# Paged softmax attention in a one-core decoder layer: values multiplied under each key block's own maximum, block weights applied in the fold

## The reference

```
gate  = q . mean(k of a block of 256 keys)      # 4 past blocks = 2 pages each
sel   = top_3(gate)  plus the query's own token
s     = q . k * 64**-0.5, masked to sel
p     = softmax(s over all chosen keys)
o     = sum(p * v)
```

## Time and profile before

| | us |
|---|---|
| median of 3 runs | 596.98 |
| lowest, highest | 594.94, 605.13 |
| the profiled execution | 596.88 |
| its span, first to last instruction | 594.9 |
| mean granted clock of PE | 0.947 of full |
| PE, DVE, ACT, POOL busy | 534.4, 350.0, 163.5, 56.6 |

### The profile page before, as it was taken

One profiled execution on the slowest core, in us unless ns is written; L12 is line 12 of the kernel. 1 busy time (PEld: TensorE's weight loads), 2 busy tenths in 40 slices (PEclk: granted clock), 3 DMA queues, 4 the chain that ended last, 5 costly groups with the idle time before them and its releaser, 6 DMA issues.

```text
span 594.9 us, 10233 instructions
## 1 busy us (share of the span) xinstructions
PE 534.4 (90%) x3943; PEld 450.2 (76%) x3943; DVE 350.0 (59%) x548; ACT 163.5 (27%) x230; POOL 56.6 (10%) x126
## 2 busy tenths in 40 slices
PE   7879997997998888988789689987999999999997
PEld 5557775675688766865564059887999999999996
DVE  4540269478798787955734537465665566455441
ACT  4101010811132122211000224364343443424420
POOL 6800010000104800000101000000000000000000
PEclk8979897997699999999969899998999999999999
DMA  9996356476049467643739998595465655645201
GB/s 294 332 302 207 108 189 218 123 204 221 19 150 324 144 221 245 217 132 119 244 111 376 384 352 268 173 298 163 148 209 162 195 169 168 195 144 193 73 19 37
DMA packets 98998, 116.79 MB, mean 196 GB/s; under 512 B 6317, under 2 KB 81278, under 8 KB 98934
## 3 DMA queue, kind: packets, MB, share of 16 engines
q1 hardware_dynamic: 93218, 104.42, 54.8%
q10 hardware_dynamic: 3908, 7.42, 3.5%
q0 software_dynamic: 1824, 4.30, 2.6%
HBM read 113.30 MB, written 2.99 MB: 195 GB/s over the span
## 4 chain that ended last, share of the span: by engine, by line
PE 64%; DVE 21%; DMA 7%; ACT 3%; issue 3%; ACTq 1%; SPq 0%; DVEq 0%
PE bank L336 61%; DVE prod L916 5%; DVE s_all L1019 5%; DVE mats L916 3%; DMA ring<-in_ada_w_dram 2%; DMA ring<-in_w_out_dram 2%; DVE BTP L916 1%; DVE cv L1127 1%; DMA ring<-in_cache_v_dram 1%; DMA x_nat<-in_x_sample_dram 1%; PE bank L373 1%; PE bank L382 1%; ACT w_part L1692 1%; DMA qb<-q_rows_dram 1%; PE bank L517 1%
## 5 line engine op out<-in xcount | busy, mean ns | idle before, releaser
L336 PE MATMUL bank<-a_hi,w_part 128*128 128x264 f32 x832 | 153.5, 286 | 2.1 <-DVE a_lo L1464 2.1
L916 DVE TENSOR_TENSOR w_part<-ring,w_part 128x2048 fp32r<-128x2048 f32 (+1 forms) x38 | 84.9, 2236 | 89.2 <-ACT w_part L1692 89.2
L336 PEld LDWEIGHTS bank<-a_hi,w_part 128*128 128x128 f32 x832 | 129.8, 189 | 2.6 <-issue 2.6
L336 PE MATMUL bank<-a_lo,w_part 128*128 128x264 f32 x416 | 118.4, 285 | 0.0
L1692 ACT ACTIVATE w_part<-ring 128x2048 fp32r<-128x2048 f32 (+1 forms) x38 | 70.9, 1871 | 86.0 <-PE bank L336 75.0
L336 PE MATMUL bank<-hT,ring 128*128 128x264 f32 x352 | 85.7, 406 | 0.8 <-ACT proj L1555 0.8
L336 PEld LDWEIGHTS bank<-hT,ring 128*128 128x128 f32 x352 | 70.0, 201 | 14.9 <-issue 2.4
L336 PEld LDWEIGHTS bank<-a_lo,w_part 128*128 128x128 f32 x416 | 79.0, 190 | 0.1
L336 PE MATMUL bank<-hid_hi,w_part 128*128 128x264 f32 x352 | 64.9, 285 | 0.0
L336 PEld LDWEIGHTS bank<-ident 128*128 128x128 f32 x362 | 48.1, 212 | 10.4 <-issue 5.6
L336 PEld LDWEIGHTS bank<-hid_hi,w_part 128*128 128x128 f32 x352 | 54.5, 188 | 0.1
(11 more groups left out here) (326 smaller groups left out, 570.3 us busy)
## 6 DMA issues: line engine op xcount, KB each, us to landing
ring<-in_ada_w_dram SPq DMA_DIRECT2D x24, 1024.0 KB, 7.3
ring<-in_cache_k_dram SPq DMA_DIRECT2D x64, 256.0 KB, 3.6
ring<-in_w_in_dram SPq DMA_DIRECT2D x11, 1024.0 KB, 5.6
ring<-in_w_gate_dram SPq DMA_DIRECT2D x11, 1024.0 KB, 5.3
ring<-in_w_up_dram SPq DMA_DIRECT2D x11, 1024.0 KB, 5.3
ring<-in_cache_v_dram SPq DMA_DIRECT2D x40, 256.0 KB, 4.2
ring<-in_w_down_dram SPq DMA_DIRECT2D x8, 1024.0 KB, 5.1
ring<-in_cache_v_dram ACTq DMA_DIRECT2D x24, 256.0 KB, 5.2
```

What stands on the lines that cost most here:

```text
L336: return pe.matmul(out, lhsT, rhs, start=start, stop=stop, skip_group_check=True)
L916: return v.tensor_tensor(out, a, b_, op)
```

## The change

The queries are handled in two groups of four. For each group, as soon as its scores exist (`G0`, `G1`), PE transposes and sums them, and DVE makes the diagonal of maxima and the blocks' gates. `DMAX0`, `DMAX1`: every block's own maximum is subtracted from its scores, with no mask and no maximum over blocks, and ACT writes the exponentials straight into the strips (`p_own`), a query's 8 columns at a place of their own in the 32. So the values of four queries gather in one bank (`pv0`, `pv1`), block by block, since a half now holds each block's first or second page. The masks and folds of `V` are gone, ACT copies each of the two banks, and ACT issues no pages. The ranking of blocks (minimum of four gates in place of counts), the maximum over blocks, the denominators and one factor for each block, query and head follow in `DEN`. `WC` turns the factors into columns, and `FO` multiplies the gathered values by them in sixteen small products that write the transposed result. In `ORDER`, `A7` moves behind `UD`, `A8` ahead of `G1` and `OWN`, and `A9` behind `V1`.

```diff
+    GS = NS // 2
+    GW = GS * NPG * H
+    XW = NPG * 32 + H
...
-             "H0 QB6 K11 L4 M4 H1 A5 H2 L5 K12 M5 A6 QB7 H3 K13 H4 L6 K14 M6 POOL H5 UA A7 K15 H6 UB UC H7 UD A8 HE OWN "
-             "A9 DMAX DEXP V0 XA V1 XB V2 XC V3 XD V4 MX V5 V6 MW0 V7 VE MD MW1").split()
+             "H0 QB6 K11 L4 M4 H1 A5 H2 L5 K12 M5 A6 QB7 H3 K13 H4 L6 K14 M6 POOL H5 UA G0 K15 H6 DMAX0 UB UC H7 UD A7 HE "
+             "A8 G1 OWN V0 DMAX1 V1 A9 XA V2 XB V3 XC V4 XD DEN V5 MX WC V6 MW0 V7 FO MD MW1").split()
...
+            def group_sums(g):
+                if g:
+                    keep_awake(6, 8)
+                pe.wait_ge(sem("k_scored"), GS * (g + 1))
+                b = opened(f"gsT{g}", (3, 6)[g])
+                for n in range(2):
+                    o = g * GW + n * P
+                    pe.transpose(b[:, GW + n * P:GW + (n + 1) * P], s_all[:, o:o + P], ident[:, :])
+                closed(mm(b[:, 0:GW], ones[:, :], s_all[:, g * GW:(g + 1) * GW]), f"gsT{g}")
+
+            def spread_max(g):
+                if g:
+                    keep_awake(5, 2)
+                pe.wait_ge(sem("max_diag"), g + 1)
+                b = opened(f"pmax{g}", (3, 5)[g])
+                closed(mm(b[:, 0:GW], ones[:, :], w_a[:, g * GW:(g + 1) * GW]), f"pmax{g}")
 
             def page_values(q):
-                if q == 0:
-                    keep_awake(4, 9)
-                    pe.wait_ge(sem("p_ready"), 1)
-                b = opened(f"pv{q}", 4 + q % 2)
+                g, j = q // GS, q % GS
+                if j == 0:
+                    pe.wait_ge(sem("p_ready"), g + 1)
+                    opened(f"pv{g}", (7, 4)[g])
+                b = bank[(7, 4)[g]]
                 for hf in range(HALVES):
                     slot = arrived(pe, ("v", (q, hf))).rearrange("p (k n) -> p k n", k=PGI)
-                    for k in range(PGI):
-                        last = mm(b[32 * k:32 * k + 32, :], pP[:, q * NPG + hf * PGI + k, :], slot[:, k, :],
-                                  hf == 0, hf == HALVES - 1)
+                    for k in range(NB):
+                        last = mm(b[32 * k:32 * k + 32, :], pP[g][:, j * NPG + PPB * k + hf, :], slot[:, k, :],
+                                  j + hf == 0, j == GS - 1 and hf == HALVES - 1)
...
+            def turn_weights():
+                pe.wait_ge(sem("wgt"), 1)
+                b = opened("wcol", 5)
+                for g in range(2):
+                    last = mm(b[:, g:g + 1], w_a[:, g * P:(g + 1) * P], ident[:, 0:1])
+                closed(last, "wcol")
+
+            def fold():
+                keep_awake(6, 6)
+                pe.wait_ge(sem("selw"), 1)
+                pe.wait_ge(sem("pv_rows"), 2)
+                b = opened("y8", 6)
+                for g in range(2):
+                    for c in range(AC):
+                        for h2 in range(2):
+                            r = 64 * h2
+                            last = mm(b[r:r + 64, c * NS + g * GS:c * NS + (g + 1) * GS],
+                                      pv_out[g][:, c * P + r:c * P + r + 64], selw[:, g, 2 * c + h2, :])
+                closed(last, "y8")
...
+            def spread_max(g):
+                b = full(v, f"pmax{g}")
+                freed(v.tensor_reduce(of(top4, g), b[:, 0:GW].rearrange("p (n t h) -> p n h t", t=PPB, h=H), AX, ALU.max),
+                      f"pmax{g}")
+                v.wait_ge(bank_free[filled[f"pmax{g}"][0]], frees_at(f"pmax{g}"))
+                s = paged(s_all[:, g * GW:(g + 1) * GW])
+                inc(tt(s, s, bc(of(top4, g).unsqueeze(2), [P, GS * NB, PPB, H]), ALU.subtract), "shifted")
+
+            def block_weights(_):
+                wide = [P, NS, NB, H]
+                low, top = sm64[:, 0, :, :], sm64[:, 1, :, :]
+                own, own_e, den, own_w = (sm64[:, n, :, :] for n in range(2, 6))
+                v.wait_ge(bank_free[filled["gsT1"][0]], frees_at("gsT1"))
+                step(v.tensor_reduce(low, over_blocks(gate4[:, :, :, :]), AX, ALU.min))
+                step(tt(cnt4[:, :, :, :], gate4[:, :, :, :], bc(low.unsqueeze(2), wide), ALU.is_le))
+                step(tt(cnt4[:, :, :, :], cnt4[:, :, :, :], bc(bidx[:, :, :].unsqueeze(1), wide), ALU.mult))
+                step(v.tensor_reduce(low, over_blocks(cnt4[:, :, :, :]), AX, ALU.max))
+                step(tt(gate4[:, :, :, :], cnt4[:, :, :, :], bc(low.unsqueeze(2), wide), ALU.is_lt))
+                step(v.tensor_scalar(cnt4[:, :, :, :], gate4[:, :, :, :], FAR, -FAR, ALU.mult, ALU.add))
+                step(tt(cnt4[:, :, :, :], cnt4[:, :, :, :], top4[:, :, :, :], ALU.add))
+                step(v.tensor_reduce(low, over_blocks(cnt4[:, :, :, :]), AX, ALU.max))
+                step(tt(top, low, own, ALU.max))
+                tt(own_e, own, top, ALU.subtract)
+                step(tt(cnt4[:, :, :, :], top4[:, :, :, :], bc(top.unsqueeze(2), wide), ALU.subtract))
+                inc(v.tensor_scalar(cnt4[:, :, :, :], cnt4[:, :, :, :], 0.0, None, ALU.min), "w_shifted")
                 b = full(v, "den")
...
+                v.wait_ge(sem("w_exp"), 1)
+                step(tt(cnt4[:, :, :, :], cnt4[:, :, :, :], gate4[:, :, :, :], ALU.mult))
+                step(tt(sum4, sum4, cnt4[:, :, :, :], ALU.mult))
+                step(v.tensor_reduce(den, over_blocks(sum4), AX, ALU.add))
+                step(tt(den, den, own_e, ALU.add))
+                step(v.reciprocal(den, den))
+                tt(own_w, own_e, den, ALU.mult)
+                for g in range(2):
+                    q = slice(g * GS, (g + 1) * GS)
+                    last = tt(w_a[:, g * P:(g + 1) * P].rearrange("p (n j h) -> p j n h", n=NB, h=H), cnt4[:, q, :, :],
+                              bc(sm64[:, 4, q, :].unsqueeze(2), [P, GS, NB, H]), ALU.mult)
+                inc(last, "wgt")
...
+            def page_exps(g):
+                a.wait_ge(sem("shifted"), g + 1)
+                a.wait_ge(sem("p_zeroed"), g + 1)
+                s = s_all[:, g * GW:(g + 1) * GW].rearrange("p (j n h) -> p j n h", n=NPG, h=H)
+                inc(a.activation(p_own[g], s, ACT.Exp, scale=SCALE), "p_ready")
...
+            def pv_rows(q):
+                if q % GS == GS - 1:
+                    take(f"pv{q // GS}", pv_out[q // GS], P, AW, "pv_rows")
...
-                    load_pages(sp, it, range(PGI // 2 if kind == "v" and i[0] >= 2 else PGI))
+                    load_pages(sp, it, range(PGI))
```

More of the change, by code:

```diff
@@ L249, in load_pages @@
             kind, (q, hf) = item
-            first = q * NPG + hf * PGI
-            pages = [eng.value_load(table[0:1, first + k:first + k + 1], min_val=0, max_val=NPHYS - 1) for k in part]
+            index = [q * NPG + (PPB * k + hf if kind == "v" else hf * PGI + k) for k in part]
+            pages = [eng.value_load(table[0:1, n:n + 1], min_val=0, max_val=NPHYS - 1) for n in index]
             if item in before:
@@ L758, in page_values @@
+                    if j < GS - 1 or hf < HALVES - 1:
                         used_up(last, ("v", (q, hf)), "pe_read")
[L759 to L772, removed]
+                if j == GS - 1:
+                    closed(last, f"pv{g}")
+                    read_by(f"pv{g}", ("v", (q, HALVES - 1)))
@@ L1333, in own_scores @@
-                step(v.tensor_scalar(g4, c4, float(min(TOPK, NB + 1)), None, ALU.is_lt))
-                step(v.tensor_scalar(c4, g4, FAR, -FAR, ALU.mult, ALU.add))
-                b = full(v, "sT")
-                freed(v.tensor_reduce(tokmax[:, :], b[:, :].rearrange("p (n t) -> p n t", n=4), AX, ALU.max), "sT")
-                v.wait_ge(bank_free[4], frees_at("sT"))
-                v.wait_ge(sem("tails_out"), 64)
-                for n in range(4):
-                    last = v.tensor_scalar(w_a[:, n * P:(n + 1) * P], ident[:, :], tokmax[:, n:n + 1], None, ALU.mult)
@@ L1353, in denominators, with of, over_blocks, group_sums @@
-            def denominators(_):
-                v.wait_ge(sem("exp8"), 1)
-                inc(tt(paged(w_b), paged(w_b), bc(g4.unsqueeze(2), [P, NS * NB, PPB, H]), ALU.mult), "exps")
+                v.wait_ge(bank_free[filled["own"][0]], frees_at("own"))
+            def of(m, g):
+                return m[:, g * GS:(g + 1) * GS, :, :].rearrange("p q n h -> p (q n) h")
+            def over_blocks(m):
+                return m.rearrange("p q n h -> p q h n")
+            def group_sums(g):
+                if g == 0:
+                    v.wait_ge(sem("tails_out"), 64)
+                b = full(v, f"gsT{g}")
+                step(v.tensor_reduce(tokmax[:, 2 * g:2 * g + 2], b[:, GW:2 * GW].rearrange("p (n t) -> p n t", n=2), AX, ALU.max))
+                for n in range(2):
+                    o = g * GW + n * P
+                    last = v.tensor_scalar(w_a[:, o:o + P], ident[:, :], tokmax[:, 2 * g + n:2 * g + n + 1], None, ALU.mult)
+                inc(last, "max_diag")
+                freed(v.tensor_reduce(of(gate4, g), b[:, 0:GW].rearrange("p (n t h) -> p n h t", t=PPB, h=H), AX, ALU.add),
```

(16 more changed lines are left out.)

162 lines of the change are left out of this document (46 added, 116 removed).

## The result

| | before | after |
|---|---|---|
| median of 4 runs, us | 597.76 | 608.97 |
| lowest, highest | 594.94, 605.13 | 607.53, 614.03 |
| the profiled execution | 596.88 | 609.32 |
| its span | 594.9 | 607.6 |
| mean granted clock of PE | 0.947 | 0.917 |

The ratio is 1.0197, with a 95% interval of 1.0147 to 1.0246: 11.2 us slower, where 10.3 us faster was predicted. The range ended at 592.5. Whether the change is more than 2% slower, this interval leaves open.

What follows compares the result with a forecast made beforehand. The bound was taken as serial: softmax weights, then value pages at full DMA rate, then masks, folds and turn. Projection start moves from 356.07 to 345.8, 10.3 us earlier, so 596.88 becomes 586.6 us; range 580.5 to 592.5.

Steps and rivals of the forecast that it cites:

- Up to K15: Group 0's work placed behind UA: K15 starts at 263.4 in place of 265.07, 1.7 us earlier.
- V0 and A9: Values and turn before XA: V0 1.93 us, 0.6 added for the clock; XA starts at 302.5, 6.0 us earlier.
- XA to the mixer's sums: Delta mixer on PE with V2 to V4 between: sums done 15.5 us after XA starts, at 318.0.
- Roots and mixer: Behind the sums: table load hidden, roots end at 318.6, mixer ready at about 323.7, 11.2 us earlier.
- rival C: Table loads wait with their activations at three places, 3 times 1.28 = 3.8 us: 590.4 us; chance 0.07.
- DEN: Ranking and weights, queued on DVE behind the mixer: 8.7 us (8.0 to 9.5), to 332.4, PE idle meanwhile.
- WC to the end of V7: PE behind the weights: WC 0.5, V6 and V7 3.86, low clock 2.6 us; V7 ends at 339.4.
- V7 to the fold: PE's 12 filling records behind V7 take 1.55 us and cover ACT's copy of pv1 (0.7).
- The fold: 32 PE records ahead of the last filling and the projection: 2.2 us (ends 1.6 and 3.8), to 343.1.
- A: The clock stays high, PE's pauses cost nothing, strided reductions go at the plain rate: 582.9 us; chance 0.20.
- D: Slower than before: after 12 us idle PE keeps the low clock through V6, V7, fold, into the projection: passes 596.9; chance 0.04.
- B: Value pages stay the bound, a half every 3.36 us, mixer 3.5 us late: 590.1 us; chance 0.14.

Runs made afterwards that it cites:

- e8: e5 with identity products that nobody reads filling PE's waits, none of them ahead of WC: 592.01 us, ratio 0.9906.
- e5: e3 with the ranking moved behind V1 and the block weights behind XB, ahead of the mixer's end: 596.88 us, ratio 0.9965.
- e1: The changed kernel with ACT again issuing half of the value pages of queries 2 to 7: 602.21 us, ratio 1.0065.
- e3: The changed kernel with the page numbers of queries 2 to 6 loaded into registers earlier, SP still issuing every page: 595.98 us, ratio 0.9954.
- e2: The kernel before with one part of the change alone, SP issuing all value pages and ACT none: 615.93 us, ratio 1.0301.
- e9: The changed kernel with the split of w_out's first part (MW0) moved behind V7: 605.81 us, ratio 1.0110.
- e10: e8 with the split of w_out's first part (MW0) moved behind V7: 591.44 us, ratio 0.9866.
- e11: e10 with ACT issuing half of the value pages of query 7: 591.91 us, ratio 0.9876.
- e12: e11 with eight identity products on PE ahead of XA and eight ahead of XC: 595.57 us, ratio 0.9935.
- e6: e3 with identity products that nobody reads filling PE's waits, 46 of them ahead of WC: 595.37 us, ratio 0.9942.

## Why the prediction was wrong

The time moved with the projection's start, as predicted (the stretch behind it 240.1 against 238.8). The start was put at 345.8 and came at 367.48, 21.7 us late. Step by step, with what each was late by:

- **Up to K15: 3.1 us, not the change's.** K14's product already starts at 250.58 where it had started at 247.47, ahead of any moved step. From K14 to K15 it took 15.75 in place of 17.60: 1.85 gained, 1.7 predicted. Later traces had the start of K15 anywhere from 262.0 (e8) to 268.7 (e5).
- **V0 and A9: 1.8 us.** V0 took 3.37 where I gave 1.93 and 0.6 for the clock. The most that I named, 1.7, was nearly what it cost (1.4).
- **XA to the mixer's sums: 10.4 us, the step that failed.** It took 25.9 us (307.38 to 333.29) where the prediction said 15.5. Two of its terms were wrong.
  - The pace of the pages: "DMA is close: 2.8 us for each half gives A9b, V2a and so on to V4b at 313.7 and V5b at 319, each just before PE wants it". The row gave what the transfers can do; what can be issued I took to be free when I wrote "ACT has no page issues left" as a pure gain. The issues didn't vanish, they moved to SP, and a half costs SP 4.25 us. The trace of before had the price: ACT's four pages at 324.07 took 4.2 us from the first number load (323.16) to the end of the last issue (327.34). PE's waits for pages are 4.0 of the 10.4 (0.92 + 1.28 + 1.81). In e1 and e3 these waits are gone (the stretch takes 22.5 and 21.8 us), which with e2 shows their cause.
  - The clock, put at nothing between XA and WC. It was low there for XA 1.3, V2 1.7, XC 0.8, V4 1.7, XD 0.7: 6.2 us. The rest of the stretch, 0.2, is rounding and small gaps. With SP relieved these 6 us are still there (e3: XA 5.78, V2 3.64, V4 3.61), and no run removed them, so what they cost in the end, and what sets them off, stays open. The prediction took a pause of about five microseconds to be needed for a low clock, since eight records behind a pause of 2.42 still took 1.07. The next row of the same list has 1.94 for eight records, behind a pause of 1.55, and the clock was at 0.50 there:

```profile
334.00:335.00 1.00, 1.00 (x8) 0.06 (x5) 0.97 (x3) 0.08 (x1) 0.00 (x0) 0.50 1.05 385
```

- **Roots and mixer: 1.3 us.** I took the table load as hidden. It stood behind its activation's wait, and the row had said so: 327.43 carries "4.17 <-PE bank". Of rival C this one load came true, the one at 335.26 ran ahead of its wait and cost nothing. The load at 332.79 took 1.28 and its activation began 0.01 us behind, as in the trace of before. The Trainium skill (ScalarE: Activation LUTs, "What ACT_TABLE_LOAD costs") counts a drain behind the load; this trace disagrees again.
- **DEN: right.** 340.16 to 349.1 is 8.9 (8.7 predicted), a strided reduction of 256 elements 0.59 to 0.61 (0.57), and PE idle 10.85 ahead of WC (about 12).
- **WC to the end of V7: right**, 7.4 against 7.0, the low clock included, with 1.0 of waiting for a page.
- **V7 to the fold: 2.9 us.** I covered the copy of `pv1` with PE's filling and overlooked what stands ahead of it on ACT. "w_out arriving after 346" was named as what would show the forecast wrong; it landed at 358.4, because SP issued it only at 351.56, behind the last page. e9 takes this back, and so do e1 and e3.
- **The fold:** 1.8 us at the low clock, 1.2 at the full one (e3: 0.64 + 0.61), 2.2 predicted. **The filling behind it:** 4.7 for 2.6, low clock again, behind the pause of 2.90.

Together 3.1 + 1.8 + 10.4 + 1.3 + 0.2 + 0.4 + 2.9 - 0.4 + 2.1 = 21.8, the 21.7 within rounding. SP's issues stand in 7.9 us of the miss (waits of 4.0 and 1.0, and the 2.9 ahead of the fold), the low clock, beyond what the forecast gave it, in 9.1 (0.8 at V0, 6.2, and 2.1 behind the fold). The two may be linked: e3, where the pause ahead of the fold is gone, has fold and filling at the full clock. Taking SP's number loads away won 13.0 us by the medians, and e3 is still 9.4 us above the forecast of 586.6.

The rivals: A, a clock that stays high, is refuted by V0, V2 and V4. D had the sign, but not the place: its low clock in V6 and V7 was already in my forecast, and there the clock came back, while the cost lay ahead of WC. B's pace, a half every 3.36 us, is near the 3.28 of e3, but not by its mechanism, as PE waited for no page of values in that stretch; and that e8, e10 and e11 end some 5 us above the forecast, close to B's time (590.1), is no support for it, since they hold other edits too. What had no rival at all was the issuing engine.

## What to carry over

When a change moves DMA issues from one queue to another, add up everything that the new queue's engine executes for each transfer, the register loads of dynamic addresses too (here 4.25 us for four pages, half again the 2.8 that I had taken for the transfer), before saying that DMA bandwidth is the limit. A wait removed from a stage that streams is worth only what the next limit leaves: in e5 13 us of waiting for DVE were gone, 5.6 us of waits for pages came, and the time was that of e3. And a small copy on an in-order engine inherits the wait of whatever was put ahead of it.

## Not expected of the hardware

- Loading one page number into a register costs SP as much as issuing the transfer: about 0.55 us a load, 0.52 an issue. Taking 40 loads out of the stretch shortened it by 11.65 us (50.97 to 39.32), 0.29 for each of them, since SP then waited 10.4 us for slots of the ring.
- The granted clock fell to 0.50 (1.2 of 2.4 GHz) within or behind XA's 64 products of 64 by 64 weights and one column in after, e8 and e12, in e12 with PE busy 3.00 of 3.00 us in the stretches before and during the fall. In the kernel before the clock had been low until 306, just ahead of XA, and stayed high through it. Filling PE's pauses gave V0 the full clock (1.92 us) and left low stretches behind XA (e6, e8, e12), and what decides their place wasn't found.
- Table loads: of three in the changed kernel that I followed, the one at 332.79 waited with its activation, the ones at 335.26 and 394.05 ran ahead of it.
